# Token shift of branch D: moved from a VectorE stage of its own to GpSimd beside the attention of branches A and B, with 12 instead of 14 gate tiles made early

## The chip, the cores and the metric

One core of one Trainium2 chip runs the whole program. The metric is the time of one execution on the device in microseconds, the median of several runs. Engines: TensorE (PE for matmuls, PEld for its weight loads), VectorE (DVE), ScalarE (ACT), GpSimd (POOL) and SyncE (SP), which issues most DMAs.

## The reference, cut to what matters

512 tokens of width 1024 go through a first block and two further layers. In the first block the input projection feeds four mixers (A and B are attentions, C a gated linear attention, D a delta rule), whose outputs are merged by sigmoid gates. The parts around the change:

```python
def _token_shift(z, mu):
    prev = jnp.pad(z, ((0, 0), (1, 0), (0, 0)))[:, :-1]
    return z + (prev - z) * mu

# first_block
    yd = _mixer_d(p["d"], ...)            # begins with seg = _token_shift(seg, mu)
    gates = jax.nn.sigmoid(p["gate"].reshape(bsz, seq, N_BRANCHES, D_MODEL))
    merged = jnp.sum(gates * jnp.einsum('bsnc,ncd->bsnd', ys, w_branch[l]), axis=2)
    x = _layer_norm(DN_ALPHA * x + merged @ w_out[l], ln_g[l, 0], ln_b[l, 0])
```

The shift acts on branch D's r, k and v (768 columns) and its low-rank inputs (64 columns). The gates are 4 x 1024 columns, in the kernel 32 tiles of 128.

## The kernel before

Activations lie with features on the 128 partitions and the 512 tokens along the free dimension, so a tile is 128x512 in fp32. Weights come as one stream of chunks, 16 blocks of 128x128 each. A block is used in a product of three matmuls: it is split in a rounded half (`hi`, ScalarE, `Stream.round`, L160) and a rest (`lo`, mostly GpSimd, `Stream.subtract`, L167), and the activations likewise; L193 to L195 are the three matmuls. The chunk after next is rounded only when TensorE starts the chunk between, by the semaphore `used`.

The program is a row of stages (`stage`). Each has its own semaphores and ends with a barrier of all engines. Inside a stage every engine follows its own order, written out by hand. The stages of the first block are: `project` (input projection into `pj`, tiles of 128 features; `T1` gives the places, with `dr`, `dk`, `dv` of two tiles each and `low` of one for branch D); `attention` for A and B, called from `mixers_ab`; `small_products`; `mixer_c` (four stages, the last of them `head_norm`); `mixer_d` (the shift stage, a stage with tanh and sigmoids, a stage with the exponents, `turn`, `delta_chunks`); `merge`.

`EarlyGates` makes part of the 32 gate tiles ahead of the merge, in places where TensorE would wait. `fill` puts matmuls on TensorE (L251, plain fp32 from `w_raw` and `res`, 8 a tile, each recorded as two), `copy` copies a finished tile from PSUM on ScalarE (L262), and `move` stores it in DRAM on SyncE (L268) and, behind each odd tile, loads the next chunk of gate weights. `EARLY_GATES` names the tiles within each half of 16 that are made early, 14 of 32 in all. Tiles 0 to 3 are made in the attention (3, 3, 2 and 0 matmuls at the end of four successive steps), 4 and 5 in `mixer_c`'s first stage, 6 in `head_norm`, 7 and 8 in the shift stage, 9 and 10 in the stage behind it, 11 to 13 in the third. The first four use PSUM bank 7, the others 6 and 7 by turns.

`attention` runs 16 steps of two units (128 queries of one head each; four steps for each pair of heads, with 128, 256, 384 and 512 keys). In step s TensorE makes the scores of step s (L881), transposes the probabilities of step s-2 (L896), multiplies with the values of step s-3 (L910) and then makes its gate matmuls. VectorE adds the bias and finds the maximum (L983, for pairs three and four after an addition at L981 also with the selection, both then in SBUF), and normalises the probabilities of step s-1 with a reciprocal and a scaling in place (L989, L990). ScalarE makes the exponentials (L937) and copies the transposes (L946). GpSimd has no work there.

The shift stage, L1478 to L1499: seven tiles, three VectorE instructions each, one after another through `Order`, while TensorE makes two gate tiles.

`merge` multiplies 32 units (one gate tile with one branch product of two blocks); a late gate is made there with 8 products of the weight stream, three gates ahead (`merge_order`), an early one is loaded by ScalarE's queue (L680) and gets its sigmoid there (L711). VectorE multiplies and adds (L752 to L759). `product_programs` with w_out follows in the same stage.

## Time and profile before

| | |
|---|---|
| median of 3 runs | 2757.49 us (2756.34 to 2758.59) |
| the profiled execution | 2755.97 us, its span 2754.2 us |
| TensorE busy | 2615.7 us, 95% |
| VectorE, ScalarE, GpSimd busy | 1072.6, 779.2, 887.9 us |
| mean granted TensorE clock | 0.969 of full |

Times in the trace count from the span's start. A row of the timeline has its start, its duration in us, engine, line and operation, the names it writes and reads, the shape and the number of instructions, and in brackets the idle time of the engine before it with the instruction that ended it. Neighbouring instructions of a kind are merged into one row. The granted clock is given as a share of full speed, 1.00 for 2.4 GHz and 0.50 for 1.2 GHz.

### The profile page before, as it was taken

The page shows a single profiled execution, that of the slowest core. Times are in us where ns is not written, and L with a number is a line of the kernel's source. Part 1 is how long each engine was busy: PE and PEld are TensorE (multiplying, and loading weights), DVE is VectorE, ACT ScalarE, POOL GpSimd, SP SyncE. Part 2 cuts the span into 40 slices and gives each one's busy share as a digit, 9 for nine tenths or more (in the row PEclk, how much of TensorE's full clock was granted, in tenths as well). Part 3 has the DMA queues.
Part 4 walks back from the last instruction along what each step waited for, and adds up shares of the span by engine and source line. Part 5 has one row for each costly group of instructions (what it writes and reads, how often), then busy time and mean ns, then how long its engine had stood idle before and what let it go on. Part 6 is the DMA issues. An engine that isn't in the chain of part 4 may idle for free. (4 is left out here: it accounts for less than half of the span.)

```text
span 2754.2 us, 30647 instructions
## 1 busy us (share of the span) xinstructions
PE 2615.7 (95%) x12344; PEld 1917.8 (70%) x12344; DVE 1072.6 (39%) x1785; ACT 779.2 (28%) x1117; POOL 887.9 (32%) x273
## 2 busy tenths in 40 slices
PE   8988789999889999899999999999999999999998
PEld 6764448788533335784888888888675888888886
DVE  4854345355231113367344411222276444411211
ACT  3023222332121112526322422322326222422311
POOL 4620000044123332230444444444320444444443
PEclk9999789899989999999999999999999999999999
DMA  4431110133469996222222222222240222222223
GB/s 166 155 120 60 46 65 1 46 115 107 199 245 389 392 391 264 86 101 27 92 94 106 92 92 97 102 92 103 104 105 15 95 95 104 92 92 98 101 92 122
DMA packets 84173, 341.56 MB, mean 124 GB/s; under 512 B 34390, under 2 KB 34774, under 8 KB 48448
## 3 DMA queue, kind: packets, MB, share of 16 engines
q1 hardware_dynamic: 64216, 316.28, 31.6%
q10 hardware_dynamic: 5992, 14.87, 1.6%
q0 software_dynamic: 13824, 8.44, 1.0%
q8 instruction: 99, 1.62, 0.2%
q14 instruction: 42, 0.34, 0.0%
HBM read 381.04 MB, written 29.79 MB: 149 GB/s over the span
## 5 line engine op out<-in xcount | busy, mean ns | idle before, releaser
L167 POOL TENSOR_TENSOR w_lo<-w_raw,w_hi 128x2048 fp32r<-128x2048 f32 x148 | 689.2, 4656 | 1541.2 <-ACT w_hi L160 1520.4
L193 PE MATMUL bank<-xh,w_hi 128*128 128x512 f32 x1752 | 697.3, 398 | 29.5 <-DVE w_lo L373 10.9
L194 PE MATMUL bank<-xl,w_hi 128*128 128x512 f32 x1752 | 687.0, 392 | 0.0
L195 PE MATMUL bank<-xh,w_lo 128*128 128x512 f32 x1752 | 686.8, 392 | 0.0
L193 PEld LDWEIGHTS bank<-xh,w_hi 128*128 128x128 f32 x1752 | 332.2, 190 | 112.9 <-issue 30.2
L160 ACT ACTIVATE w_hi<-w_raw 128x2048 fp32r<-128x2048 f32 x150 | 286.4, 1909 | 360.5 <-PE bank L193 338.7
L194 PEld LDWEIGHTS bank<-xl,w_hi 128*128 128x128 f32 x1752 | 332.0, 189 | 73.2 <-issue 5.0
L195 PEld LDWEIGHTS bank<-xh,w_lo 128*128 128x128 f32 x1752 | 331.9, 189 | 69.3
L193 PE MATMUL bank<-ha,w_hi 128*128 128x512 f32 x480 | 186.7, 389 | 0.0
L194 PE MATMUL bank<-hb,w_hi 128*128 128x512 f32 x480 | 186.7, 389 | 0.0
L195 PE MATMUL bank<-ha,w_lo 128*128 128x512 f32 x480 | 186.7, 389 | 0.0
L2992 DVE TENSOR_TENSOR yb<-bank,mats 128x512 f32<-128x512 f32 x64 | 44.3, 692 | 205.8 <-PE bank L195 205.8
L251 PE MATMUL bank<-res,w_raw 128*128 128x512 f32 x224 | 110.7, 649 | 1.9 <-PEq L293 1.9
L3028 DVE TENSOR_TENSOR yb<-yb,bank 128x512 f32<-128x512 f32 x44 | 30.2, 687 | 203.3 <-PE bank L195 203.3
L2958 ACT ACTIVATE yb<-yb 128x512 f32<-128x512 f32 x64 | 40.4, 632 | 241.4 <-DVE yb L2992 241.4
L193 PEld LDWEIGHTS bank<-ha,w_hi 128*128 128x128 f32 x480 | 90.1, 188 | 18.8
L195 PEld LDWEIGHTS bank<-ha,w_lo 128*128 128x128 f32 x480 | 90.1, 188 | 18.7
L194 PEld LDWEIGHTS bank<-hb,w_hi 128*128 128x128 f32 x480 | 90.1, 188 | 18.4
L2138 PE MATMUL bank<-ring,xt 128*64 128x512 f32 x392 | 96.1, 595 | 0.0
L3025 DVE TENSOR_TENSOR yb<-bank,mats 128x512 f32<-128x512 f32 x44 | 30.4, 692 | 156.7 <-PE bank L195 144.1
L251 PEld LDWEIGHTS bank<-res,w_raw 128*128 128x128 f32 x224 | 44.9, 206 | 60.4 <-issue 60.3
L2974 ACT ACTIVATE ha<-yb 128x512 fp32r<-128x512 f32 x44 | 27.8, 632 | 204.7 <-DVE yb L3028 204.7
(581 smaller groups left out, 3549.4 us busy)
## 6 DMA issues: line engine op xcount, KB each, us to landing
w_raw<-weights SPq DMA_DIRECT2D x189, 1024.0 KB, 4.8
ring<-weights SPq DMA_DIRECT2D x49, 1024.0 KB, 10.1
before_halves<-weights SPq DMA_DIRECT2D x18, 1024.0 KB
res<-weights SPq DMA_DIRECT2D x16, 1024.0 KB
distance_bias<-distance_bias_once ACTq DMA_DIRECT2D x8, 512.0 KB
na_bias<-grid_bias SPq DMA_DIRECT2D x16, 240.0 KB, 6.4
strips<-distance_bias SPq DMA_DIRECT2D x8, 448.0 KB, 3.8
early_gates<-gate_rows SPq DMA_DIRECT2D x14, 256.0 KB, 2.0
```

Of the source, the lines that this page charges most:

```text
L160: act.activation(self.hi[:, s, :], self.raw[:, s, :], ACT.Copy).then_inc(self.rounded, 1)
L167: engine.tensor_tensor(self.lo[:, s, :], self.raw[:, s, :], self.hi[:, s, :].bitcast(F32), ALU.subtract).then_inc(self.split, 1)
L193: self.released(pe.matmul(out, hi, moving[0], start=start, stop=False))
L194: pe.matmul(out, hi, moving[1], start=False, stop=False)
L195: return pe.matmul(out, lo, moving[0], start=False, stop=stop)
L251: mm = pe.matmul(self.k.bank[self.banks[j]][:, :], self.k.ws.raw[:, c % 2, 128 * (b % 16):128 * (b % 16) + 128], self.k.res[:, t, :], star ...
L2138: last = pe.matmul(out[side_rows[side], :], xt[:, b % 3, columns_of(t, side)], g[:, SEQ * (t % 4):SEQ * (t % 4) + SEQ], start=t == 0, stop ...
L2958: act.activation(sig[:, u % 3, :], sig[:, u % 3, :], ACT.Sigmoid).then_inc(sigmoid_ready, 1)
L2974: act.activation(fh[:, j, :], mid, ACT.Copy).then_inc(row_rounded, 1)
L2992: dve.tensor_tensor(sig[:, u % 3, :], k.bank[u % 4][:, :], k.rstd, ALU.mult).then_inc(gate_scaled, 1)
L3025: dve.tensor_tensor(silu[:, j % 2, :], ffn_bank(j, 0)[:, :], k.rstd, ALU.mult).then_inc(act_scaled, 1)
L3028: dve.tensor_tensor(mid, silu[:, j % 2, :], ffn_bank(j, 1)[:, :], ALU.mult).then_inc(lin_read, 1)
```

## The change

The shift becomes a function `shift` that `mixers_ab` gives to `attention`, and GpSimd runs it in that stage. It has four instructions for a tile instead of three (the multiply-add is split into a scaling by `mu` and an addition), a buffer `moved` of its own, and touches 96 rows of the tile `low` instead of 128. Each instruction waits for the one before it through the semaphore `pool_order`. The shift stage of `mixer_d` goes, with its two gate tiles. The sigmoid table that it loaded is loaded at the end of `head_norm`. `EARLY_GATES` has six places instead of seven, so 12 gate tiles are made early and 20 late, and the order of the weight stream follows.

```diff
-EARLY_GATES = (0, 2, 4, 7, 9, 11, 14)
+EARLY_GATES = (0, 2, 5, 8, 10, 13)
...
+        if shift:
+            @block.gpsimd
+            def _(pool):
+                shift(pool, Order(pool, pool_order))
...
             if gates:
+                act.preload_act_table_set("sigmoid_and_others")
                 gates.copy(act, 1)
...
-    with memory(k, strips=(4, STRIP)) as strips:
+    with memory(k, strips=(4, STRIP), moved=(SEQ,)) as (strips, moved):
+        def shift(pool, step):
+            for j, t in enumerate([T1["dr"], T1["dr"] + 1, T1["dk"], T1["dk"] + 1, T1["dv"], T1["dv"] + 1, T1["low"]]):
+                rows = slice(0, 96 if t == T1["low"] else 128)
+                z, sh, mu = pj[rows, t, :], moved[rows, :], k.par1[rows, P1["mu"] + j:P1["mu"] + j + 1]
+                step(pool.tensor_tensor(sh[:, 1:SEQ], z[:, 0:SEQ - 1], z[:, 1:SEQ], ALU.subtract))
+                step(pool.tensor_scalar(sh[:, 0:1], z[:, 0:1], -1.0, None, ALU.mult))
+                step(pool.tensor_scalar(sh, sh, mu, None, ALU.mult))
+                step(pool.tensor_tensor(z, sh, z, ALU.add))
...
-        with stage(k, "vector_order") as (block, order):
-            @block.tensor
-            def _(pe):
-                k.gates.fill(pe, 16)
-
-            @block.scalar
-            def _(act):
-                act.preload_act_table_set("sigmoid_and_others")
-                k.gates.copy(act, 2)
-
-            @block.sync
-            def _(sp):
-                k.gates.move(sp, 2)
-
-            @block.vector
-            def _(dve):
-                step = Order(dve, order)
-                for j, t in enumerate([R, R + 1, K_, K_ + 1, V, V + 1, T1["low"]]):
-                    z = pj[:, t, :]
-                    step(dve.tensor_tensor(sh[:, 1:SEQ], z[:, 0:SEQ - 1], z[:, 1:SEQ], ALU.subtract))
-                    step(dve.tensor_scalar(sh[:, 0:1], z[:, 0:1], -1.0, None, ALU.mult))
-                    step(dve.scalar_tensor_tensor(z, sh, p1("mu", j), z, ALU.mult, ALU.add))
```

## Rows read from the trace of the kernel before

**Rows 1.** The page's first part: busy time, share, instructions.
```profile
PE 2615.7 (95%) x12344; PEld 1917.8 (70%) x12344; DVE 1072.6 (39%) x1785; ACT 779.2 (28%) x1117; POOL 887.9 (32%) x273
```

**Rows 2.** The table of stretches: stretch, length, busy time of each engine.
```profile
core 0: us, PE busy (x) PEld busy (x) DVE busy (x) ACT busy (x) POOL busy (x), PEclk, DMA share, GB/s
177.00:257.00 80.00, 69.73 (x370) 35.74 (x371) 35.80 (x140) 34.20 (x104) 0.00 (x0) 0.94 0.24 86
324.19:341.79 17.60, 15.67 (x32) 6.54 (x32) 11.17 (x21) 2.43 (x3) 0.00 (x0) 0.90 0.26 90
550.00:680.00 130.00, 128.43 (x567) 106.06 (x566) 72.65 (x73) 39.44 (x46) 56.18 (x12) 1.00 0.35 118
```

**Rows 3.** Timeline around the shift stage: start, duration, instruction, idle time before.
```profile
322.28 0.60 ACT L262 ACTIVATE gate_rows<-bank 128x512 f32<-128x512 f32 x1 [3.72 <-PE bank L251]
...
324.15 1.28 ACT L1485 ACT_TABLE_LOAD   x1 [1.27 <-PEq L293]
...
324.19 15.67 PE L251 MATMUL bank<-res,w_raw 128*128 128x512 f32 x32 [1.95 <-PEq L293]
...
341.79 0.63 ACT L1505 ACTIVATE tl<-pj 16x512 f32<-16x512 f32 x1 [1.30 <-ACTq L293]
```

**Rows 4.** Timeline of ScalarE in the merge, and a row of the waits there.
```profile
571.10 1.92 ACT L160 ACTIVATE w_hi<-w_raw 128x2048 fp32r<-128x2048 f32 x1 [7.96 <-PE bank L193]
...
581.98 1.92 ACT L160 ACTIVATE w_hi<-w_raw 128x2048 fp32r<-128x2048 f32 x1 [7.47 <-PE bank L193]
...
PE bank L193 <- DVE yl L744: 1.6, 1, 1.6
```

**Rows 5.** Timeline of GpSimd and VectorE where both work.
```profile
562.22 4.61 POOL L167 TENSOR_TENSOR w_lo<-w_raw,w_hi 128x2048 fp32r<-128x2048 f32 x1 [7.92 <-ACT w_hi L160]
...
564.12 0.69 DVE L752 TENSOR_TENSOR part<-ahead,bank 128x512 f32<-128x512 f32 x1 [4.20 <-PE bank L195]
564.84 2.55 DVE L758 TENSOR_TENSOR part<-part 128x512 f32<-128x512 f32 x1
...
68.14 4.79 POOL L150 TENSOR_TENSOR w_lo<-w_raw,w_hi 128x2048 fp32r<-128x2048 f32 x1
...
70.70 2.52 DVE L1242 TENSOR_SCALAR yb<-yb 128x512 f32<-128x512 f32 x1
```

**Rows 6.** Groups of GpSimd's instructions by form: count, busy, mean ns, idle.
```profile
L150 POOL TENSOR_TENSOR w_lo<-w_raw,w_hi 128x2048 fp32r<-128x2048 f32 x12 | 55.7, 4643 | 0.9
L147 POOL TENSOR_TENSOR w_hi<-w_raw,w_zero 128x2048 fp32r<-128x2048 f32 x12 | 44.0, 3666 | 42.5 <-PE bank L193 40.2 <-PE bank L201 2.2
...
L2072 POOL MEMSET work<- 128x3072 f32 x1 | 2.7, 2658 | 45.3 <-DVE res L570 45.3
```

**Rows 7.** Attention: a row of the waits, then timelines of three engines.
```profile
PEld bank L896 <- DVE att_p L990: 8.5, 4, 3.3
...
191.33 0.42 DVE L990 TENSOR_SCALAR att_p<-att_p,att_s 128x384 f32<-128x384 f32 x1
...
191.54 0.63 ACT L946 ACTIVATE yb<-bank 128x256 f32<-128x256 f32 x2
...
192.04 0.85 PE L896 MATMUL bank<-consts,att_p 128*128 128x128 f32 x6 [1.32 <-ACT yb L946]
```

**Rows 8.** TensorE in the attention, and a stretch with its granted clock.
```profile
228.11 0.85 PE L896 MATMUL bank<-consts,att_p 128*128 128x128 f32 x6 [2.05 <-ACT yb L946]
229.47 4.54 PE L251 MATMUL bank<-res,w_raw 128*128 128x512 f32 x6
...
236.40 2.84 PE L251 MATMUL bank<-res,w_raw 128*128 128x512 f32 x6
...
229.00:234.00 5.00, 5.00 (x16) 1.99 (x16) 0.49 (x1) 1.73 (x7) 0.00 (x0) 0.66 0.14 52
```

**Rows 9.** TensorE's gate matmuls in branch D's next stage, and the stretch.
```profile
347.51 16.54 PE L251 MATMUL bank<-res,w_raw 128*128 128x512 f32 x32
...
343.00:353.00 10.00, 9.22 (x19) 3.64 (x20) 3.99 (x6) 3.12 (x6) 0.00 (x0) 0.52 0.00 0
```

More of the change, by code:

```diff
@@ L835, in root_programs, with attention @@
     return names, dict(tensor=tensor, scalar=scalar, scalar_end=scalar_end, vector=vector)
-def attention(k, units, outs, probt, strip_loads=(), gates=None, kept=None):
+def attention(k, units, outs, probt, strip_loads=(), gates=None, kept=None, shift=None):
     steps = len(units) // 2
@@ L851, in attention @@
                   "out_copied", "vector_order", "strip_in0", "strip_in1", "strip_in2", "strip_in3", "kept_squared",
-                  "kept_summed", "kept_log", "kept_rstd") as (
+                  "kept_summed", "kept_log", "kept_rstd", "pool_order") as (
                 block, scores_ready, biased, exp_ready, probs_ready, turned, turned_copied, unit_done, out_copied,
-                order, strip_in0, strip_in1, strip_in2, strip_in3, kept_squared, kept_summed, kept_log, kept_rstd):
+                order, strip_in0, strip_in1, strip_in2, strip_in3, kept_squared, kept_summed, kept_log, kept_rstd,
+                pool_order):
         strip_in = (strip_in0, strip_in1, strip_in2, strip_in3)
@@ L1298, in mixers_ab @@
                               select=select[:, i - 1, 0:n] if b and i else None, rows=rows, cols=tiles[i]))
-        attention(k, units, [yb[:, p, :] for p in range(4)], yb[:, 4:8, :], strip_loads=loads, gates=k.gates)
+        attention(k, units, [yb[:, p, :] for p in range(4)], yb[:, 4:8, :], strip_loads=loads, gates=k.gates,
+                  shift=shift)
     small_products(k, [(yb[:, 2 + p, :], k.mats1[:, 256 + 128 * p:384 + 128 * p], yb[:, 2 + p, :], None)
```

## The prediction

> **What bounds the kernel now.** I read the page's first part, then the table of stretches, then the timeline of each stage that the change touches. TensorE is busy for 95% of the span [rows 1]. Three stretches matter [rows 2]. In the attention of branches A and B (177 to 257 us) TensorE is busy 69.7 of 80 us, VectorE 35.7, ScalarE 34.2, and GpSimd not at all. The shift stage of branch D lasts 17.60 us, TensorE busy 15.67. In the merge (550 to 680 us) TensorE is busy 128.4 of 130 us at full clock: each further product there lengthens the kernel. After the merge TensorE stays bound up to the end, so what is won or lost ahead of it reaches the end at face value. All this is one execution of 2755.97 us; the median of the three timed runs is 2757.49, 1.5 us more. I add differences to the median.
>
> **The stage that goes.** In the stage ahead of it ScalarE copies its gate tile at 322.28 us; then comes a barrier, and the shift stage starts with a table load at 324.15 and two gate tiles on TensorE (32 records, 15.67 us) from 324.19; the next stage starts with ScalarE's tanh at 341.79 [rows 3]. VectorE's 21 instructions take 11.2 us of it and end first: the stage is as long as its two gate tiles. The boundary before it (from 322.28 + 0.60 to 324.15, 1.27 us) and the one behind it (idle 1.30) are alike, so what goes is 341.79 - 324.19 = 17.60 us. The gate tiles of later stages keep their banks (7, then 6 and 7 by turns, and tiles 7 and 9 are both odd), and each chunk is still loaded behind an odd tile, one stage ahead of its use. The table load moves behind the last Exp of head_norm and ahead of its gate copy, where ScalarE is idle 3.72 us for TensorE (the idle time ahead of the copy at 322.28) [rows 3]; its 1.28 us lie in there, cost nothing, and would cost 1.28 without that cover. SyncE loses two stores and one load of early gates, ScalarE two loads in the merge: nothing waits for them now.
>
> **Two gate tiles come late.** A late gate is 8 products of three matmuls, so two are 16 products, one whole chunk. While TensorE never waits, ScalarE rounds a chunk each time TensorE starts the next: 571.10 and 581.98, 10.88 us apart [rows 4]. The merge gains 10.88 us. Its only wait of note, 1.6 us for yl [rows 4], lies at the second branch product; the first units are in the same order as before, and so it stays. The gates behind it lie further apart (0, 2, 5, 8, 10, 13), so VectorE has more time for each unit; the last branch products before w_out are four with no gate between them, not five, so its backlog is smaller. GpSimd's splitting (one 4.6 us instruction per chunk) stays hidden, one chunk more of it. I put zero on the rest of the merge, bounds -0.3 to +1.
>
> So far: -17.60 + 10.88 = -6.72 us.
>
> **GpSimd beside the attention.** The trace has no shift on GpSimd. Its nearest rows are [rows 6]: 4.64 us for 128x2048 with two full inputs, 3.67 us with one full input and one broadcast column, and 2.66 us for a memset of 3072 columns. A quarter of the first two is 1.16 and 0.92 us for 512 columns. Per tile I take 1.2 + 0.15 + 0.9 + 1.2 and four waits of 0.08 us, about 3.8 us, and 7 tiles are 26.5 us. From 177.0 that ends at 203.5, some microseconds later where VectorE holds it up. Bounds: by the memset (0.44 us for 512 columns) a third less for the scalar step and 23 us in all; if each instruction kept half of the long ones' time, 7 x (2.3 + 0.15 + 1.8 + 2.3) = 46 us. Either is hidden in 80 us. Nobody waits for the result before branch D, and nothing is queued behind it on GpSimd before the merge. Its direct cost is zero; if it took over 80 us the block's end would wait for it.
>
> **What it does to VectorE.** This is the real price. At 564.84 us an addition with both inputs in SBUF (0.69 us alone) took 2.55 us and ended at 567.39, after GpSimd's instruction of 562.22 + 4.61 = 566.83 [rows 5]. The product just before it, one input from PSUM, took its usual 0.69 us under the same instruction. At 70.70 a multiplication with one SBUF input took 2.52 us and ended behind GpSimd's of 68.14 + 4.79 = 72.93. So VectorE stands still, for the rest of GpSimd's running instruction, with two SBUF inputs and also with a plain SBUF-to-SBUF scaling. In the attention that is the normalisation at L990, twice in each of 16 steps, and from the third pair of heads the selection at L983. The biased scores (one input in PSUM) go free.
>
> A GpSimd instruction leaves on average 0.5 us when VectorE arrives (half of the squares' sum over 3.8 us of cycle) and at most 1.2; the second L990 of a step meets the next one and waits 0.7 more. So each step of VectorE under GpSimd becomes about 1.2 us longer, at most 2.4. Does TensorE feel it? It waited for L990 at four places, those steps that have no gate matmuls between, the count in the wait's row [rows 7]. The first is at 192.0: the second L990 of the pair ended at 191.75, ScalarE's copy started at 191.54 and ended its first half near 192.0, and TensorE started at 192.04. The transposes of the second unit come some 0.4 us after those of the first, so about 0.65 us of 1.2 is slack: 0.6 us lost, bounds 0 to 1.9. In the steps before it VectorE is idle 1 to 2 us, which covers the mean and not the maximum; I add 0.3. Steps with gate matmuls have several microseconds of room. The next such place is at 208, past my end of GpSimd.
>
> A second effect is the clock. At 228.11, after an idle time of 2.05 us, TensorE's granted clock fell soon: the six gate records at 229.47 took 4.54 us where the same six at 236.40 took 2.84, and the stretch 229 to 234 has 0.66 [rows 8]. After the idle 1.32 us at 192.04 it stayed at full. If the wait there grows to two microseconds the fall may come here too: 1.7 us. I give it 4 in 10, hence 0.7. With 0.4 for the chance that GpSimd is still at work at 208, the attention costs 2.0 us; bounds 0 (all hidden) and 6 (two places at 1.9 + 1.7, and some rest).
>
> The Trainium skill (SBUF — State Buffer, "Who interferes with whom") says that whoever issues first holds the shared port pair for its whole instruction and that the other blocks fully, for two SBUF inputs and for the two-port modes of tensor_scalar; the trace agrees (2.55 for 0.69 us). The same skill (GPSIMD Engine Reference, "Elementwise — side-by-side cycle accounting") puts a one-input loop at about 1.8 cycles per element and a two-input one at 2.6; by it the chain would be an estimated 25 us, and the sum the same.
>
> **The stage behind the removed one.** It starts at half clock (1.2 GHz, not 2.4): 0.52 of full from 343 to 353 [rows 9]; its two gate tiles take 16.54 us against about 13.7 at full. It will stand after a shorter busy stretch and at another instant. Nearest rows for how long a half-clock spell lasts here are 3.4 us (229 to 234 at 0.66, so 0.34 x 5 x 2) and 9.6 us (343 to 353 at 0.52). The first end would gain up to 3 us; the other way it could lose 2. I take zero.
>
> **Sum.** -17.60 + 10.88 + 2.0 + 0 = -4.7 us: 2751.3 in terms of the profiled execution, 2752.8 us in terms of the median.
>
> **The rivals.**
> - *Nothing is paid in the attention*, or the half-clock spells fall well: -6.7 and down to -9, so 2750.8 to 2748.5. For: VectorE is idle over half of the attention, and 0.65 us of the wait are slack. Against: two-input rows that grew fourfold. Chance 0.33.
> - *The gain is eaten*: GpSimd's instructions carry a fixed part, the chain takes 40 to 50 us, and two or three of the ungated places are hit, each at 1.9 us and a clock fall of 1.7: +4 to +8 us, net -2.7 to +1.3, 2754.8 to 2758.8. For: no row has a short GpSimd instruction with two inputs. Against: only two of the four places lie before 223. Chance 0.22.
> - *Slower than before*: the chain outlasts the attention. At more than 80 / 7 = 11.4 us for a tile the block waits at its end; with the selection of pairs three and four blocked too (four blocked instructions a step), +4 to +8 us come before that. To be 5.5 us slower the sum has to reach 12.2: a chain of some 86 us, 12.3 us for a tile. That is three times my price. Chance 0.05.
> - *The early gates were not what the stage hid*: the removed tiles cost 7.8 us each there and 5.44 in the merge, so moving them costs nothing more than counted; that the merge hides them is excluded by its full TensorE.
>
> **How the numbers follow.** Forecast -3 to -6: 0.40; the cheap case 0.33; the eaten one 0.22; the slower 0.05. A measurement of this kernel tells about 0.2% (5.5 us) from no change. Faster than that: the cheap case whole and 0.04 of the forecast, 0.37. Within: 0.58. Slower: 0.05. The range runs from 2748.5 (-9) to 2757.5 (0), leaving out 0.05 below and 0.13 above.
>
> **What would show it.** The next stage of D starting 17.6 us earlier less the attention's cost; GpSimd ending at 203 to 207; L990 rows of 1 to 1.7 us in the first seven steps and as before later; 16 more products in the merge and 10.9 us between the same marks; no new wait of TensorE there. I am wrong if the short GpSimd instructions take 2 us, if TensorE waits where gate matmuls should cover, or if the clock falls at 192.

## The result and the profile after

| | before | after |
|---|---|---|
| timed side by side, median (range), 5 runs each | 2757.49 us (2756.17 to 2758.59) | 2741.05 us (2740.05 to 2743.81) |
| ratio after / before | | 0.9945, interval 0.9930 to 0.9961 |
| profiled execution, its span | 2755.97, 2754.2 us | 2741.05, 2739.3 us |

The change gained 16.4 us where I forecast 4.7; the time lies 7.4 us below the low end of my range. The experiments show that this comparison was a lucky one, and say by how much: over 101 executions of the kernel before and 11 of the changed one the difference of the means is 12 us.

The page of the changed kernel, its part on busy time (engine, busy us, share of the span, instructions), against [rows 1]:

```profile
PE 2600.1 (95%) x12360; PEld 1914.3 (70%) x12360; DVE 1067.9 (39%) x1764; ACT 779.6 (28%) x1116; POOL 921.0 (34%) x302
```

TensorE has 16 instructions more and yet is busy 15.6 us less (2615.7 before). Part of that is the kind of work: 32 records that took 15.67 us in the removed stage [rows 3] went, and the rest of the merge is busy 10.67 us longer (162.87 for 152.20 below), so 5.0 us less. The other 10.6 us fell at unchanged work, which points at the clock. So I cut both traces into stretches at the same instructions. First the changed kernel, a table of stretches (stretch, length, busy time and count of PE, PEld, DVE, ACT, POOL, then the granted clock as a share of 2.4 GHz, the DMA share and GB/s). In order: attention; small products and branch C up to the norm; head norm (in the kernel before with the shift stage); D's tanh stage; D's exponent stage; the start of the merge (three rounds of ScalarE); the rest of the merge from its fifth round; everything behind it.

```profile
178.69:259.05 80.36, 69.08 (x369) 35.40 (x369) 39.22 (x140) 34.20 (x104) 28.91 (x28) 0.94 0.24 86
259.05:311.99 52.94, 38.64 (x155) 23.96 (x155) 19.62 (x35) 7.44 (x13) 0.00 (x0) 0.74 0.09 30
311.99:322.77 10.78, 8.85 (x20) 3.71 (x20) 2.89 (x4) 7.32 (x10) 0.00 (x0) 1.00 0.04 16
322.77:345.56 22.79, 18.88 (x44) 7.76 (x44) 9.52 (x14) 5.49 (x9) 0.00 (x0) 0.85 0.20 70
345.56:372.61 27.05, 24.30 (x57) 10.59 (x57) 14.57 (x26) 10.27 (x18) 0.00 (x0) 1.00 0.08 32
505.32:535.68 30.36, 27.91 (x107) 20.32 (x108) 22.35 (x23) 17.05 (x22) 4.85 (x1) 0.95 0.37 139
546.56:711.34 164.78, 162.87 (x719) 134.54 (x717) 68.82 (x71) 40.61 (x42) 65.14 (x14) 1.00 0.25 88
711.34:2739.30 2027.96, 1962.43 (x9182) 1439.27 (x9182) 705.62 (x1095) 598.34 (x795) 721.16 (x231) 0.98 0.38 138
```

The same stretches in the profiled execution of the kernel before on which my prediction rests:

```profile
177.04:256.19 79.15, 68.92 (x368) 35.24 (x369) 35.80 (x140) 34.20 (x104) 0.00 (x0) 0.94 0.25 87
256.19:311.72 55.53, 41.08 (x154) 26.34 (x154) 19.63 (x35) 7.43 (x13) 0.00 (x0) 0.69 0.08 29
311.72:341.79 30.07, 26.18 (x52) 10.93 (x52) 14.06 (x25) 8.63 (x11) 0.00 (x0) 0.89 0.17 59
341.79:366.00 24.21, 20.28 (x44) 8.20 (x44) 9.52 (x14) 5.50 (x9) 0.00 (x0) 0.79 0.18 66
366.00:394.54 28.54, 25.79 (x56) 11.24 (x57) 14.56 (x26) 10.39 (x18) 0.00 (x0) 0.94 0.08 30
527.45:560.22 32.77, 30.63 (x107) 22.09 (x108) 22.34 (x23) 17.05 (x21) 4.83 (x1) 0.85 0.34 129
571.10:725.18 154.08, 152.20 (x671) 125.50 (x669) 66.28 (x71) 39.35 (x41) 61.09 (x13) 1.00 0.27 91
```

Read line against line: in five of the seven stretches of the kernel before (all but the third and the last) TensorE's counts are the same to one record, so its part of those lines can differ only in clock and waits. The tanh stage, the exponent stage and the start of the merge have 44, 57 (one of them without a record before) and 107 matmuls in both kernels, and each is shorter as its clock is higher: 0.85 for 0.79, 1.00 for 0.94, 0.95 for 0.85. The differences in us, after less before: start of the attention +1.65, attention +1.21, up to the norm -2.59, head norm and shift stage -19.29, tanh -1.42, exponents -1.49, turn and delta rule -0.20, start of the merge -2.41, its rest +10.70, all behind it -1.06: together -14.9. The two terms that I had worked out from instructions are there, -19.29 (with 1.7 of clock in it) and +10.70. The +1.65 ahead of the attention is no effect of the change: in the eight profiles of the kernel before the attention starts anywhere from 174.8 to 182.5 us, in the two of the changed kernel at 178.7 and 176.2.

### The profile page after: what moved, and what is told of

The parts are those of the page before. It is cut to its first block and busy times, and to the rows that moved or that the text cites. A ratio compares the mean times of both kernels' runs of the same rounds, so it can differ in the third digit from the quotient of the medians.

```text
span 2739.3 us, 30663 instructions
## 1 busy us (share of the span) xinstructions
PE 2600.1 (95%) x12360; PEld 1914.3 (70%) x12360; DVE 1067.9 (39%) x1764; ACT 779.6 (28%) x1116; POOL 921.0 (34%) x302
## 5 line engine op out<-in xcount | busy, mean ns | idle before, releaser
L2986 DVE TENSOR_TENSOR yb<-bank,mats 128x512 f32<-128x512 f32 x64 | 44.3, 692 | 205.7 <-PE bank L195 205.7
L251 PE MATMUL bank<-res,w_raw 128*128 128x512 f32 x192 | 92.0, 631 | 0.0
L3019 DVE TENSOR_TENSOR yb<-bank,mats 128x512 f32<-128x512 f32 x44 | 30.4, 691 | 156.8 <-PE bank L195 144.1
L796 DVE TENSOR_TENSOR yb<-bank,mats 128x512 f32<-128x512 f32 x16 | 11.1, 691 | 188.9 <-PE bank L195 188.9
## 6 DMA issues: line engine op xcount, KB each, us to landing
res<-weights SPq DMA_DIRECT2D x16, 1024.0 KB, 14.3
```

Source lines behind the costliest of these rows:

```text
L251: mm = pe.matmul(self.k.bank[self.banks[j]][:, :], self.k.ws.raw[:, c % 2, 128 * (b % 16):128 * (b % 16) + 128], self.k.res[:, t, :], star ...
L2986: dve.tensor_tensor(sig[:, u % 3, :], k.bank[u % 4][:, :], k.rstd, ALU.mult).then_inc(gate_scaled, 1)
L3019: dve.tensor_tensor(silu[:, j % 2, :], ffn_bank(j, 0)[:, :], k.rstd, ALU.mult).then_inc(act_scaled, 1)
```

## The experiments

Each kernel was timed beside the kernel before on the same chip. A "spell" is a stretch at 0.50 of full clock; those up to 740 us last from 3.4 to 23.9 us. "Level" is one of two groups into which the times of the kernel before fall: the upper level is 2753.8 us and more, the lower one 2743.1 to 2750.6 us.

### Both kernels once more, unchanged

> The kernel before, once more, for a second profile of it. Clock theory (the 10 us beyond my sum are half-clock spells of TensorE that fall on less work): 2757 us; the spells before 560 us cover about 90 us as in the first profile (105 us up to 760) if their places belong to the kernel, or differ by 10 us and more between the two profiles if they are chance. Structure theory (the whole 16 us belong to removed and moved work): the same places and the same 2757 us, and nothing of the rest depends on them.

> The changed kernel once more. Clock theory: 2741 us, and half-clock spells with some 20 us less in all than in the kernel before, in the stages of branch C and the start of the merge, where the code is the same. If the spells were chance of single executions, this profile would show other places and the time would spread by 5 us.

Measured: the kernel before 2755.18 us (2746.52 to 2759.53, 10 runs), its twin of the same minutes 2743.14 to 2762.27 (26 runs); the changed kernel 2741.47 (2737.50 to 2744.57, 6 runs), ratio 0.9954 (0.9938 to 0.9971). The difference is real, and the changed kernel keeps its time. But the kernel before scatters over 19 us, in two heaps. So the comparison above had caught only the upper heap. By means the gain is 11.8 us here.

The second profile of the kernel before has the stretches of the first to 0.1 us, except for the time before the attention (1.2 us more) and that behind the merge (1.4 us less). The second profile of the changed kernel differs from its first one where the code is the same: branch C lasts 54.96 us for 52.94 and the head norm 12.43 for 10.78, each at a lower clock (0.69 and 0.86, for 0.74 and 1.00), while the tanh stage (22.77), the exponent stage (27.04) and the start of the merge (30.34) are as short as in the first. The fourth column of the table further down has the differences of this pair.

### The shift left out, and the shift moved with the stage kept

```diff
 # no_shift: GpSimd does nothing in the attention; the token shift is left out of the computation
-        attention(k, units, [yb[:, p, :] for p in range(4)], yb[:, 4:8, :], strip_loads=loads, gates=k.gates,
-                  shift=shift)
+        attention(k, units, [yb[:, p, :] for p in range(4)], yb[:, 4:8, :], strip_loads=loads, gates=k.gates)
```
```diff
 # stage_kept: shift on GpSimd, but the old stage with its two gate tiles stays, without VectorE; 14 early gates
-            @block.vector
-            def _(dve):
-                step = Order(dve, order)
...
```

> The changed kernel with the token shift left out altogether (branch D works on unshifted values): GpSimd idle in the attention. My prediction: 2.0 us less than the changed kernel, between 0 and 6, all of it in the attention. Clock theory: the attention is about 1 us shorter, but the total moves by anything from -5 to +5 us, since all later work meets the spells elsewhere. Structure theory: -1 to -2 us, no more.

> The shift on GpSimd beside the attention, but the stage of branch D kept with its two gate tiles on TensorE, and 14 early gates as before. Only VectorE's 21 instructions are gone from that stage, which ends with TensorE. My prediction: 2757.5 + 2.0 = 2759.5 us. Structure theory, if the shift itself was what cost: clearly below 2757. Clock theory: 2757 +-5 us, with the difference from the kernel before made of half-clock spells.

Measured: without the shift 2744.12 us (2738.35 to 2747.78, 9 runs), ratio 0.9966 (0.9952 to 0.9981), that is 2.7 us above the changed kernel, not below. The work on GpSimd costs the whole kernel nothing that can be measured; the attention lasts 79.82 us in the profile of no_shift, and 80.36 and 79.58 in the two of the changed kernel. With the stage kept 2752.41 (2745.36 to 2755.95, 10 runs), ratio 0.9986 (0.9972 to 1.0), 3.0 us below the median beside it: the move of the shift alone gains little or nothing, since the stage was as long as its gate tiles. The rest of the gain comes with the removed stage, but not by its instructions alone: stage_kept lies 10.9 us above the changed kernel, and -17.6 + 10.7 are 6.9. In its profile the tanh stage, the exponent stage and the start of the merge last 23.19, 28.53 and 32.78 us, 4.3 us more in all than in the changed kernel (22.79, 27.05, 30.36).

### Half a microsecond of idle time ahead of the tanh stage

```diff
 # after_pad05: one copy on ScalarE that nobody reads, ahead of the tanh stage's first instruction
-    with memory(k, tl=(SEQ,), zs=(2, 4)) as (tl, zs):
+    with memory(k, tl=(SEQ,), zs=(2, 4), pad=(2, SEQ)) as (tl, zs, pad):
...
+                act.activation(pad[:, 0, :], k.res[:, 0, :], ACT.Copy)
 # after_pad16: three such copies
```

> The changed kernel with one idle ScalarE copy (0.53 us) ahead of the tanh of branch D's first remaining stage; all later work comes 0.53 us later against the instants at which TensorE's granted clock changes. Structure theory (the gain is the removed stage): +0.5 us, so 2742.0. Clock theory: in the kernel before the spell in that stage ended 10.9 us behind the stage's start, in the changed one 8.0; modulo the 3.4 us that the shortest spell lasts these are 0.65 and 1.2 us. A delay of 0.53 makes 0.7 of the 1.2, so the stages should get the lengths of the kernel before: 24.2, not 22.8 us for the first, 28.5, not 27.05 for the next, 32.8, not 30.35 at the merge's start: +0.5 + 1.4 + 1.5 + 2.4 = +5.8 us, 2747.

> The same with three copies (1.6 us). Structure theory: +1.6 us, 2743. Clock theory: the end of the spell comes to 1.2 - 1.6 + 3.4 = 3.0 us, where the kernel with the kept stage has it (23.2, 28.5 and 32.8 us for the three): +1.6 + 0.4 + 1.5 + 2.4 = +5.9 us, 2747. If both theories are wrong the three lengths stay at 22.8, 27.05 and 30.35 whatever the delay.

This was the test of the clock theory. Table of stretches of after_pad05, the tanh stage, the exponent stage and the start of the merge:

```profile
325.35:349.51 24.16, 20.27 (x44) 8.20 (x44) 9.52 (x14) 5.48 (x10) 0.00 (x0) 0.79 0.17 62
349.51:378.06 28.55, 25.80 (x56) 11.24 (x57) 14.56 (x26) 10.38 (x18) 0.00 (x0) 0.94 0.08 30
510.99:543.75 32.76, 30.61 (x107) 22.13 (x108) 22.34 (x23) 17.04 (x21) 4.84 (x1) 0.85 0.34 129
```

These are the kernel before's three lengths (24.21, 28.54, 32.77) and clocks (0.79, 0.94, 0.85) to a few hundredths, in a kernel that differs from the changed one by a single copy of 0.6 us. Where TensorE stands inside the first of them shows in the timeline of its gate matmuls (start, duration, instruction), first the changed kernel, then after_pad05; [rows 9] has the kernel before with 16.54:

```profile
328.49 15.14 PE L251 MATMUL bank<-res,w_raw 128*128 128x512 f32 x32
```
```profile
331.05 16.53 PE L251 MATMUL bank<-res,w_raw 128*128 128x512 f32 x32
```

And the spell at the start of the tanh stage, from the table of stretches of the changed kernel and of after_pad05:

```profile
324.00:330.80 6.80, 6.05 (x15) 2.44 (x16) 1.38 (x2) 2.74 (x6) 0.00 (x0) 0.50 0.01 4
```
```profile
326.00:336.20 10.20, 8.89 (x18) 3.44 (x19) 3.65 (x6) 3.66 (x6) 0.00 (x0) 0.50 0.01 2
```

It lasts 10.2 us instead of 6.8, as in the kernel before (342.4 to 352.7), a spell of 3.4 us comes back in the exponent stage, and the one at the merge is 20.5 us instead of 13.7. In time: 2746.75 us (2743.25 to 2755.04, 12 runs), ratio 0.9978 (0.9965 to 0.9992), 5.3 us above the changed kernel's 2741.47 for 0.6 us of work (on another chip; the kernel before has medians of 2755.13 and 2755.45 us on the two). The profiled execution, at the slow end, is 11.5 us longer in span than that of the changed kernel: 5.3 us are in the three stretches, 0.6 is the copy, 2.2 lie ahead of the attention and 3.5 behind the merge. Three copies (after_pad16) gave 2748.85 (2740.89 to 2752.24, 12 runs), ratio 0.9985 (0.9973 to 0.9997), with a tanh stage of 23.65 and the start of the merge at 32.68, but the exponent stage at 27.04, at full clock as in the changed kernel: the three spells are not one thing, and the arithmetic with which I had expected 28.5 there failed.

### The kernel before with the idle time made longer

```diff
 # before_pad29: five and a half copies on ScalarE that nobody reads, ahead of the tanh stage's first instruction
+                act.activation(pad[:, 0, :], k.res[:, 0, :], ACT.Copy)
...
+                act.activation(pad[:, 5, 0:256], k.res[:, 5, 0:256], ACT.Copy)
```

> The kernel before with 2.9 to 3.0 us of idle copies ahead of the same tanh. Structure theory: +2.9 us, slower by 0.1%. Clock theory: 0.65 - 2.9 + 3.4 = 1.15 us, which is where the changed kernel has it, so the three lengths become 22.8 + 2.9, 27.05 and 30.35 and the kernel gets 5.3 - 2.9 = 2.4 us faster although it does 2.9 us more.

Measured: 2756.16 us (median of 12 runs, 2746.25 to 2758.63 but for one of 5302.81), ratio 1.0002 (0.9987 to 1.0018). The pad lengthened its place by 2.8 us (norm to tanh 32.89 for 30.07), and the kernel is not longer: the start of the merge went from 32.77 to 30.29, as in the changed kernel. But the tanh stage (24.37) and the exponent stage (28.65) did not become shorter, against what I expected. So the kernel before can have the short start of the merge too; that the pad brought it is not shown, for in one of the eight profiles of the kernel before (before_again1, below) it came by itself:

```profile
533.13:563.45 30.32, 27.77 (x107) 20.34 (x108) 22.35 (x23) 17.06 (x22) 4.85 (x1) 0.95 0.39 139
```

The other two I could not steer, and no rule for where a spell ends follows from these runs.

### Fourteen early gates without the stage

```diff
 # gates14
-EARLY_GATES = (0, 2, 5, 8, 10, 13)
+EARLY_GATES = (0, 2, 4, 7, 9, 11, 14)
...
-                k.gates.fill(pe, 24)
+                k.gates.fill(pe, 40)
```

> The changed kernel with 14 early gates at their places of before: the two tiles of the removed stage are made in the stage with the exponents, behind its three. By my sum: two tiles there cost 2 x 6.86 = 13.7 us, for TensorE ends that stage, and the merge gets 10.88 us shorter: +2.9 us, 2744.4. If a gate tile in the merge cost more than 5.44 us (a loss by order or by VectorE that I put at zero), this kernel would come out at or below the changed one. The clock may add or take a few us in both theories; the lengths of the two stages in the trace settle it.

Table of stretches of gates14, the exponent stage and the merge from its fifth round:

```profile
345.10:385.88 40.78, 38.04 (x89) 16.67 (x89) 14.56 (x26) 11.46 (x20) 0.00 (x0) 1.00 0.16 60
562.47:716.55 154.08, 152.17 (x671) 125.50 (x669) 66.30 (x71) 39.35 (x42) 61.12 (x13) 1.00 0.26 91
```

Two more gate tiles with nothing to hide behind cost 40.78 - 27.05 = 13.73 us there and save 164.78 - 154.08 = 10.70 in the merge: +3.0. The timed runs say 2745.26 (2741.39 to 2748.88, 11 runs), 3.8 above the changed kernel. They do not confirm the 3.0 by themselves: in the profile the start of the merge has the long spell again (to the end of the fourth round 43.7 us for 41.2), 2.5 us that the sum does not hold. The lengths of the two stretches, both at full clock, are the evidence. A gate tile made early in plain fp32 costs 6.9 us at full clock, a late one 5.35 us. That is 3.0 of the 6.9 us by which 17.60 exceeds 10.70. The rest is that the stage held 1.9 us in which TensorE was idle (17.60 - 15.67) and ran its tiles below full clock (15.67 for 13.73 us, at 0.90 by [rows 2]). Both ways make the same tiles, and the late way is cheaper unless the early one fills a wait.

### The shift done twice

```diff
 # shift_twice: in each tile, once more, into a buffer that nobody reads
                 step(pool.tensor_tensor(z, sh, z, ALU.add))
+                step(pool.tensor_tensor(sh[:, 1:SEQ], z[:, 0:SEQ - 1], z[:, 1:SEQ], ALU.subtract))
+                step(pool.tensor_scalar(sh[:, 0:1], z[:, 0:1], -1.0, None, ALU.mult))
+                step(pool.tensor_scalar(sh, sh, mu, None, ALU.mult))
+                step(pool.tensor_tensor(unused[rows, :], sh, z, ALU.add))
```

> The changed kernel with GpSimd's four instructions done a second time in each tile, the second result into a buffer that nobody reads, so that the chain lasts about 63 us instead of 31.3 us and ends near 241 us, still before its first reader at about 323 us. Theory (the chain costs the attention by single VectorE divisions held up, of which only those at the step from one pair of heads to the next reach TensorE): two more pair steps may be met, at about 1 to 1.3 us each, so the attention lasts 80.4 to 83 us against 80.36, and the whole is 1 to 3 us above the changed kernel (2741.5), give or take 3 for where the half-clock spells fall. Rival (GpSimd's work holds VectorE up in proportion to its busy time, the case that my prediction called the eaten gain): the attention lasts 84 to 88 us and the whole is 4 to 8 us above the changed kernel.

Table of stretches of shift_twice, the attention, and its row of the waits (us in total, times, longest):

```profile
179.57:260.93 81.36, 68.98 (x369) 35.74 (x369) 46.34 (x140) 34.21 (x104) 59.63 (x56) 0.94 0.24 85
```
```profile
PEld bank L897 <- DVE att_p L996: 11.4, 8, 3.3
```

GpSimd works 59.63 us of the 81.36, VectorE is busy 46.34 us instead of 39.22 in the changed kernel and 35.80 before, and TensorE waits 11.4 us for the normalisation instead of 9.9 in the changed kernel and 8.5 before [rows 7]. The attention is 1.0 us longer than in the first profile of the changed kernel, 1.8 longer than in the second. The theory's 80.4 to 83 us holds for it; the rival's 84 to 88 does not. The whole is 2740.87 us (2738.59 to 2742.40, 7 runs), the changed kernel's time: inside the theory's give or take, below the rival's 4 to 8 us more. That equality is no measure of GpSimd's price, for the spells fell elsewhere. Branch C up to the norm, the tanh stage and the exponent stage of shift_twice:

```profile
260.93:309.64 48.71, 34.26 (x154) 22.28 (x155) 19.64 (x35) 7.32 (x13) 0.00 (x0) 0.82 0.09 33
320.43:344.77 24.34, 20.43 (x44) 8.29 (x44) 9.52 (x14) 5.49 (x9) 0.00 (x0) 0.79 0.19 66
344.77:373.40 28.63, 25.88 (x56) 11.23 (x57) 14.57 (x26) 10.38 (x18) 0.00 (x0) 0.94 0.08 30
```

Branch C is 4.2 and 6.3 us shorter than in the two profiles of the changed kernel, and D's two stages are as long as in the kernel before (+3.1 us), though the code of these stages is the changed kernel's. So the short D stages do not belong to the changed code either. Against the "eaten gain" stands the attention: even at twice the dose it grew by 1.0 to 1.8 us, not by 4 to 8.

### A few gate matmuls ahead of the waits

```diff
 # fills_first: tanh stage; the same with 1 of 24 in the exponent stage and 1 of 8 in head_norm
             def _(pe):
+                k.gates.fill(pe, 2)
...
-                k.gates.fill(pe, 16)
+                k.gates.fill(pe, 14)
```

> The changed kernel with a few of the gate matmuls that the stages of branch D hand to TensorE put ahead of the waits on the activations instead of all behind them: 2 of 16 in the tanh stage, 1 of 24 in the exponential stage, 1 of 8 in the stage with the head norm. They use the idle time of TensorE's first wait in each stage. Theory: each stage's idle at its start shrinks by the length of the matmuls put there, 1.7 + 0.7 + 0.8 us by the idle seen in the changed kernel, so 2.5 to 3 us less than the changed kernel, 2739, if no half-clock spell moves onto these stages. Rival (how idle time and full clock go together decides more than the instructions do): the time is within 2 us of the changed kernel, or above it, with the segments at the starts of the stages shorter and a spell elsewhere longer.

Table of stretches of fills_first, tanh stage, exponent stage and the start of the merge:

```profile
323.59:346.63 23.04, 21.09 (x44) 8.19 (x45) 9.52 (x14) 5.50 (x10) 0.00 (x0) 0.78 0.20 69
346.63:372.98 26.35, 24.27 (x56) 10.57 (x57) 14.56 (x26) 10.27 (x18) 0.00 (x0) 1.00 0.08 32
506.65:539.36 32.71, 30.55 (x107) 22.07 (x108) 22.35 (x23) 17.05 (x22) 4.85 (x1) 0.86 0.35 129
```

The exponent stage is 0.7 us shorter as planned. The tanh stage is not: its idle time went from 3.9 to 2.0 us, and its clock from 0.85 to 0.78 (a spell of 10.2 us for 6.8). Here the spell grew although TensorE stood still for less time. The start of the merge is 2.35 us longer, at 0.86. The third place shows no gain either: the stretch from the head norm to the tanh lasts 10.79 us for 10.78 although one gate matmul was put ahead of it, at 0.91 instead of full clock. In all 2743.06 us (2736.91 to 2751.20, 11 runs), ratio 0.9964 (0.9947 to 0.9980): the rival holds, and this is no better version.

### The kernel before, in search of its lower level

> The kernel before once more, unchanged. The timed runs of it lie in two clusters, about 2744 to 2750 us and about 2753 to 2762 us, and the profiled executions so far were of the second. Theory (the half-clock spells fall on other work from one execution to the next and make both the clusters and what the change gained over its instruction count): if this execution is one of the first cluster, its mean granted clock is near 0.973 against 0.969, the half-clock time before 560 us is 10 us or more below 104 us, and the segments that get shorter are ones in which a spell no longer lies, with the instruction counts unchanged. Rival (the clusters come from the transfers or from the chip): the spells lie where they lay (291.2 to 315.1, 342.4 to 352.7, 516.5 to 537.0) and the segments differ elsewhere.

> As the run before this one: the kernel before, unchanged, for a second chance at an execution of the faster cluster. If both are of the slower cluster (2753 us or more), nothing is told apart, and where the faster cluster's spells lie stays open.

> The kernel before, unchanged, in search of an execution of its lower level of time (2744 to 2750 us). Theory: there the half-clock spells between 290 and 560 us are shorter by about 15 us in all (the one from 291 to 315 is 13.7 us long, or the one of the stage behind the removed one is 6.8, or the one from 517 to 537 is 13.7), and the segments that hold them are shorter by half of the busy part. Rival: the spells before 760 us are as they were, and the difference lies behind the merge or in segments at full clock. At the upper level nothing is told.

The fourth to the sixth were told the same as the third:

> As before_again3: the kernel before, unchanged, for another chance at its lower level of time.

> As before_again3: the kernel before, unchanged, for another chance at its lower level of time.

> As before_again3: the kernel before, unchanged, for another chance at its lower level of time.

Measured: 2759.33, 2757.23, 2753.31, 2749.24, 2745.91 and 2744.06 us; the last three are of the lower level, and their spells agree but for one or two short ones. Table of stretches of before_again6, from the attention to the start of the merge, to be laid beside the two tables at the top:

```profile
177.24:254.49 77.25, 67.22 (x368) 34.55 (x369) 35.78 (x140) 34.21 (x104) 0.00 (x0) 0.96 0.25 89
254.49:303.65 49.16, 34.32 (x154) 22.49 (x154) 19.62 (x35) 7.32 (x13) 0.00 (x0) 0.83 0.09 33
303.65:332.06 28.41, 24.52 (x52) 10.29 (x52) 14.06 (x25) 8.53 (x12) 0.00 (x0) 0.94 0.17 62
332.06:356.14 24.08, 20.18 (x44) 8.20 (x44) 9.52 (x14) 5.50 (x9) 0.00 (x0) 0.79 0.19 65
356.14:384.65 28.51, 25.76 (x57) 11.22 (x57) 14.56 (x26) 10.38 (x18) 0.00 (x0) 0.94 0.08 30
517.54:550.32 32.78, 30.65 (x107) 22.10 (x108) 22.33 (x23) 17.05 (x22) 4.84 (x1) 0.85 0.35 129
```

The same program, instruction for instruction, is 6.4 us shorter in branch C (49.16 for 55.53), 1.9 in the attention and 1.7 in the head norm, each at a higher clock; a spell of 6.8 us in branch C (260.5 to 267.3 in the upper level) is missing, and the one from 291.2 to 315.1 ends after 13.7 us. The last three lines are those of the upper level: D's stages and the start of the merge are as in the upper level. The same holds for the fourth and the fifth (branch C 49.17 and 49.13, attention 77.45 and 77.64). The third run, with 2753.31 us, has the upper level's stretches (79.14, 55.64) and is short because its attention starts at 174.8 us. My theory held, but half of its expectation did not: I had named the tanh stage and the start of the merge among the candidates.

Of all 101 executions of the kernel before, parted by their mean clock, 35 have 0.972 to 0.974 and 2743.1 to 2750.6 us (mean 2747.5), 61 have 0.969 to 0.970 and 2753.8 to 2762.3 us (mean 2757.3; four of the first comparison, whose clock is not on record, are counted here by their time), and 5 have 0.971 and 2749.3 to 2753.3 us. The 11 of the changed kernel lie between 2737.5 and 2744.6, mean 2741.6, clock 0.973 to 0.975.

## Why the prediction was wrong, step by step

Changed kernel less kernel before, in us:

| stretch | forecast | first profiles (upper level) | second profiles (same_after less same_before, upper level) | first changed less before_again6 (lower level) |
|---|---|---|---|---|
| start of the attention | 0 | +1.65 | -2.07 | +1.45 |
| attention | +2.0 | +1.21 | +0.42 | +3.11 |
| small products, branch C | 0 | -2.59 | -0.64 | +3.78 |
| head norm and shift stage | -17.60 | -19.29 | -17.59 | -17.63 |
| tanh stage, exponent stage | 0 | -2.91 | -2.88 | -2.75 |
| turn, delta rule | 0 | -0.20 | -0.12 | -0.18 |
| start of the merge | 0 | -2.41 | -2.45 | -2.42 |
| rest of the merge | +10.88 | +10.70 | +10.67 | +10.72 |
| all behind | 0 | -1.06 | +0.48 | +0.92 |
| sum | -4.7 | -14.9 | -14.2 | -3.0 |

**The stage that goes: right.** -17.59 and -17.63 in the two pairs in which the head norm itself lasts alike in both kernels; in the first pair the kernel before takes 1.7 us more there (12.47 for 10.78), at a lower clock. The table load moved where I said and is hidden; ScalarE in the changed kernel, from its timeline (start, duration, instruction, idle before):

```profile
317.51 1.28 ACT L1126 ACT_TABLE_LOAD   x1
320.87 0.60 ACT L262 ACTIVATE gate_rows<-bank 128x512 f32<-128x512 f32 x1 [2.08 <-PE bank L251]
322.77 0.63 ACT L1499 ACTIVATE tl<-pj 16x512 f32<-16x512 f32 x1 [1.30 <-PEq L293]
```

Behind the load ScalarE still waited 2.08 us for TensorE; of the 3.72 of [rows 3] the load took 1.28 and more was not needed.

**Two late gates: right.** 10.67 to 10.72 us against 10.88 from the distance of two rounds [rows 4]; the rest of the merge at zero holds as well, and gates14 turned the term back.

**GpSimd's chain: a size was off.** I took 3.8 us for a tile and 26.5 us in all; it took 4.5 and 31.3. The timeline of GpSimd, from the first tile and around 191:

```profile
178.68 1.04 POOL L1290 TENSOR_TENSOR moved<-pj 128x511 f32<-128x511 f32 x1 [18.97 <-POOLq L293]
179.81 0.23 POOL L1291 TENSOR_SCALAR moved<-pj 128x1 f32<-128x1 f32 x1
180.14 1.58 POOL L1292 TENSOR_SCALAR moved<-moved,par 128x512 f32<-128x512 f32 x1
...
190.80 1.27 POOL L1293 TENSOR_TENSOR pj<-moved,pj 128x512 f32<-128x512 f32 x1
192.15 1.04 POOL L1290 TENSOR_TENSOR moved<-pj 128x511 f32<-128x511 f32 x1
...
208.70 1.26 POOL L1293 TENSOR_TENSOR pj<-moved,pj 96x512 f32<-96x512 f32 x1
```

The subtraction and the addition are near my 1.2 us. The scaling by a column is not the cheap one: 1.6 us where I took 0.9 from a quarter of L147 [rows 6], which is no scaling but the addition of a broadcast column of zeros. The Trainium skill (GPSIMD Engine Reference, "Elementwise — side-by-side cycle accounting") gives 1.8 cycles an element as the best case of a tight loop and 2.6 for two inputs, and I had read the first as the price of the scaling. The trace does not bear that out: 1.6 us with one full input, 1.04 to 1.27 us with two.

**VectorE's blocking: right in kind, too dear.** I expected the normalisation to take 1 to 1.7 us in the first seven steps. Its whole time in the attention rose only from 12.4 to 15.8 us for 32 instructions, and only four single ones came near 1 us (in the second profile two, of 1.30 and 1.01). The worst pair of them and TensorE behind it:

```profile
191.27 1.02 DVE L996 TENSOR_SCALAR att_p<-att_p,att_s 128x384 f32<-128x384 f32 x1
...
192.40 1.01 DVE L996 TENSOR_SCALAR att_p<-att_p,att_s 128x384 f32<-128x384 f32 x1
```
```profile
192.52 0.52 PE L897 MATMUL bank<-consts,att_p 128*128 128x128 f32 x3 [1.32 <-ACT yb L947]
193.46 0.55 PE L897 MATMUL bank<-consts,att_p 128*128 128x128 f32 x3 [0.42 <-DVE att_p L996]
```

Both ran under two-input instructions of GpSimd (190.80 and 192.15 above) and each ended 0.22 us behind the end of it. At this place TensorE waited 0.42 us between the two halves of its transposes, which ran in one piece before [rows 7]. I had put 0.6 us there. The clock did fall behind it, at 194.3 to 197.7, which I had given 4 chances in 10: the next transposes come 7.1 us behind these (199.58), where they came 4.8 us behind in the kernel before (196.81). In the second profile of the changed kernel neither the wait nor the fall came. The attention is 1.21 us longer than in the upper level in the first profile and 0.42 in the second, with three spells of 3.4 us in each (178.6, 229.8, 250.3 before; 194.3, 231.8, 252.3 in the first profile after), so the direct price was 0.4 to 1.2 us against my 2.0. Without any shift the attention lasted 79.82 us, between the two (no_shift); in the time of the whole kernel no price can be seen.

**The clock of the stages behind: this step failed.** "I take zero", with bounds -3 to +2, looked at one spell, that of the tanh stage, and at no others. That stage alone stayed within the bounds, with -1.4 us. The exponent stage with -1.5 and the start of the merge with -2.4 had no term at all; together the three are -5.3 us in both pairs of profiles. In the tanh and the exponent stage all eight profiles of the kernel before, of both levels, have a longer spell than the two of the changed kernel, at the start of the merge seven of the eight. All three were back in after_pad05, with one copy of 0.6 us more, and two of them in shift_twice, whose D stages are untouched. So they come from where the work falls in time and in what pattern, and from nothing that the change did to the work itself. What in that pattern decides is open: longer idle time gave the long spell in after_pad05, shorter idle time gave it in fills_first.

**The level of the kernel before: a step that was missing.** The trace that I read showed one of two ways in which the same program runs, 10 us apart, and three timed runs within 2.3 us gave no hint of it. Against the lower level the mean gain is 5.9 us, against all 101 executions 12.0, against the upper level, which the first comparison met in all its runs, 15.7 us. My -4.7 is nearest to the first, but not by its own reasons alone: in the lower level's column of the table the spells give back 3.8 us in branch C and part of the 3.1 in the attention, and take 5.2 in the stages of branch D and at the merge. What stands free of them is the arithmetic of instructions, -17.6 + 10.7 and +0.4 to +1.2 in the attention, -5.7 to -6.5. With the -5.3 of the step before that makes -11 to -12, near the mean gain of 12.0. The further 4.4 us of the first comparison were luck, the luck of meeting the upper level alone. Why the changed kernel kept to one level in its 11 executions (7.1 us from end to end), while no_shift, after_pad05 and fills_first spread over 9.4, 11.8 and 14.3 us (shift_twice over only 3.8), is open too: one changed program happened to fall well, and I can show no property of it that makes it so. What parts the two levels of the kernel before is known only as far as where the spells lie, not why.

**The rivals.** "Nothing is paid, or the half-clock spells fall well" was the side on which it came out, for its second reason; I had let it reach only to -9. "The gain is eaten" is refuted by the attention, which grew by 0.4 to 1.2 us where the rival had 4 to 8, and by no more than 2.2 with the shift done twice. "Slower, the chain outlasts the attention" fell with the chain of 31.3 us. The range was built from the bounds of the priced edits; the spread of the kernel itself, known only after many runs, was larger than all of them.

## What to carry to other kernels

Cut both traces at the same instructions and look for stretches with equal counts and unequal length: their granted clock tells at once what no sum of instructions will. A kernel with half-clock spells at its many short idle times has a time that depends on where they fall; here the median with one copy of 0.6 us more lay 5 us higher, so a forecast of a change that shifts work in time needs some 5 us on both sides for that alone, and the kernel before needs ten runs or more ahead of any forecast of a few us. Filler work is worth its place only while it fills a wait: the early gate tile cost 6.9 us where TensorE had nothing to wait for and 5.35 us in the merge. Removing the stage paid by that, by the stage's own idle time of 1.9 us and by its tiles' lower clock, not by freeing VectorE.

## What the runs showed of the hardware

- One program, unchanged, ran at two levels, 2747.5 and 2757.3 us on the mean, with mean granted clocks of 0.973 and 0.969, on each chip where it was timed often; the difference in the profiles lies in spells at 1.2 GHz between 177 and 332 us.
- One of VectorE's scalings from SBUF to SBUF was not held to the end of GpSimd's one-input scaling, only slowed: it took 0.63 us for 128x512, against 0.49 alone, and ended at 194.56, inside the instruction of 193.60 + 1.57. The next, of 0.78 us from 194.67, ended behind that instruction. Under two-input instructions they were held to the end (1.02 for 0.42). The timeline of VectorE there:

```profile
193.93 0.63 DVE L996 TENSOR_SCALAR att_p<-att_p,att_s 128x512 f32<-128x512 f32 x1
```

- GpSimd scaled 128x512 by a column in 1.57 to 1.64 us, more than an addition of two full inputs (1.26 to 1.32 us), and a single column took 0.22 to 0.23 us.
